# A gated delta rule layer: the last level of a block inverse in 32x32 tiles

## The chip, the cores and the metric

The kernel runs on one core of a Trainium2 chip. The metric is the device time of one execution in microseconds (us). The core has a matrix engine (PE, with its weight loads shown as PEld), a vector engine (DVE), a scalar engine (ACT), GpSimd (POOL) and a sync engine whose queue (SP) starts most transfers. Each engine works through its own list of instructions in order; engines wait for each other on semaphores.

## The reference, cut to what matters

One layer: a modulated RMS norm, one wide projection, an attention half (8 heads), a gated delta rule half (4 heads of 128), and an output projection with a gated residual. 256 tokens, float32. The change touches the delta rule alone, which works on chunks of 64 tokens:

```
sys = A + eye(64)                        # A strictly lower triangular, per head and chunk
u = solve(sys, v * beta)                 # = T (v beta),     T = inverse of sys
w = solve(sys, kb * exp(G))              # = T (kb exp G)
def step(state, xs):                     # over the 4 chunks, state starts at zero
    v_new = u_c - w_c @ state
    o     = q_c @ state + qk_c @ v_new
    state = state * gl + k_c.T @ v_new
```

For the first chunk the state is zero, so `w_c @ state` is zero and w of that chunk is used nowhere.

## The kernel before, in words

Every engine has an order of calls written out by hand; nothing is planned at run time. Tokens stand in two tiles (t = 0, 1) of 128, each with two chunks (c = 0, 1) on partitions 0 to 63 and 64 to 127. For heads 2 and 3 the two chunks of a tile stand in exchanged places; `side(h, c)` gives the partitions of chunk c of head h.

T is built by doubling blocks of 1, 2, 4, ..., 32 (`LEVELS = 6`, levels 0 to 5). `tt` holds the transpose of T as far as it is known, `am` the transposed A, `ti` the 32x32 blocks of `tt` turned on DVE. At level l and tile t:

- PE `z_products` (L1630): A times the odd blocks of T, 4 heads x 2 chunks, each with 64 contracted rows, 64 loaded columns and 32 streamed columns, into bank 2 + 2t;
- DVE `mask_z` (L1079): product with a 0/1 mask (read from `cst`) into `zt`, 128 partitions x 4 heads x 32;
- DVE `turn` (L1066): turns `tt` into `ti`;
- PE `x_products` (L1641): `ti` times `zt`, the same shapes, into the other half of the bank;
- DVE `merge` (L1086): subtracts the result from the odd blocks of `tt`.

The next level of the same tile waits for `merge` (semaphore t_done). The two tiles take turns. After level 5 come `w_products(0)`, `w_products(1)` (L1652, `kw` times `tt`, 64 contracted rows, 128 loaded and 64 streamed columns), the copies of their results by ACT (`wT_copy`, L704) and `u_products(0)` (L1666), which writes a bank that `wT_copy(0)` has to have read. Then PE goes on with units of the wide projection (`half(11)`, `half(12)`; L1395 to L1397). A product of f32 operands is issued as two MATMUL instructions, so a group of 4 heads x 2 chunks has 16.

The order around the change on PE is `x_products(4, 1)`, `z_products(5, 0)`, `z_products(5, 1)`, `x_products(5, 0)`, `x_products(5, 1)`, `w_products(0)`, `w_products(1)`, `u_products(0)`, `half(11)`, `half(12)`, `state_products(0)` (L1714), `scores(2)` (L1738). On DVE it is `merge(4, 1)`, `mask_z(5, 0)`, `turn(5, 1)`, `mask_z(5, 1)`, `merge(5, 0)`, `merge(5, 1)`, `rope(2)` (L1097, L1098, L1101), `gated_heads(1)` (L1141), `gate_sums(0, 0, 4)` (L1157), `rope(3)`, `lo(31)` (L915), `maxima(2)` (L1119, L1122), `gate_sums(0, 4, 8)`. `turn(5, 0)` stands ahead of `merge(4, 1)`. `scores(2)` waits for `rope(3)`.

Of the kernel before, what the change touches and what calls it, by code (L numbers as in the profile page):

```python
# [32 lines left out]
ACT = mybir.ActivationFunctionType  # L33
ALU = mybir.AluOpType
# [9 lines left out]
DH, DK = 4, 128  # L44
DW = DH * DK
CHUNK = 64
# [18 lines left out]
LEVELS = 6  # L65
HALF = CHUNK // 2
# [15 lines left out]
def build(nc, x, x_turned, ada, gate_w, gate_b, post_w, w_qkv, w_rest, w_gates, w_out, const, out):  # L82
    with ExitStack() as ctx:
# [73 lines left out]
        def th_array(name):  # L157
            return sb(name, [P, NTH, P])
        kw, kd, vb = th_array("kw"), th_array("kd"), th_array("vb")
        def th_block(name, n=CHUNK):  # L160
            return sb(name, [P, NTH, n])
        dec = sb("dec", [P, 2, NTH, CHUNK])
        am, qkd, qd = th_block("am"), th_block("qkd"), th_array("qd")
        ti, tt = th_block("ti"), th_block("tt")
        zt = th_block("zt", HALF)
        with ExitStack() as e:
            sq = sb("sq", [P, 4, 512], into=e)
        wT, vnew = th_array("wT"), kw
# [35 lines left out]
        z_ready, z_masked, ti_done, x_ready, t_done, wT_ready, wT_copied = map(  # L204
            sem, ("z_ready", "z_masked", "ti_done", "x_ready", "t_done", "wT_ready", "wT_copied"))
# [45 lines left out]
        def heads(a, t):  # L251
            return a[:, t * DH:(t + 1) * DH, :]

        def odd(ap, l):
            return ap.rearrange("p (n two b) -> p n two b", two=2, b=1 << l)[:, :, 1, :]

        def heads_odd(a, t, l):
            return heads(a, t).rearrange("p h (n two b) -> p (h n) two b", two=2, b=1 << l)[:, :, 1, :]

        def blocks(b, o, n):  # L260
            return bank[b][:, o:o + DH * n].rearrange("p (h j) -> p h j", h=DH)

        def rows_of(c):
            return slice(c * CHUNK, (c + 1) * CHUNK)

        def side(h, c):
            return rows_of(c if h < 2 else 1 - c)
# [4 lines left out]
        def ident_of(c):  # L272
            return ident[rows_of(c), rows_of(c)]
# [8 lines left out]
        ACROSS = (0, 2, 1, 3)  # L282
# [247 lines left out]
        def _(act):  # L530
# [169 lines left out]
            def wT_copy(t):  # L700

                act.wait_ge(wT_ready, t + 1)
                for c in range(2):
                    act.activation(heads(wT, t)[:, :, rows_of(c)], blocks(2 + 2 * t + c, 0, CHUNK), ACT.Copy, scale=-1.0).then_inc(wT_copied, 1)  # L704

            def vnew_copy(n):
                act.wait_ge(vnew_ready, n + 1)
# [109 lines left out]
            hi(29)  # L817
            hi(30)
            wT_copy(0)
            wT_copy(1)  # L820
            vnew_copy(0)
            hi(31)
# [37 lines left out]
        def _(dve):  # L860
# [215 lines left out]
            def mask_z(l, t):  # L1076

                dve.wait_ge(z_ready, NT * (l - 1) + t + 1)
                dve.tensor_tensor(heads(zt, t), blocks(2 + 2 * t, 0, HALF),  # L1079
                                  cst[:, C_LV + l * HALF:C_LV + (l + 1) * HALF].unsqueeze(1).to_broadcast([P, DH, HALF]), ALU.mult).then_inc(z_masked, 1)  # L1080

            def merge(l, t):

                dve.wait_ge(x_ready, NT * (l - 1) + t + 1)
                x_t = blocks(2 + 2 * t, 256, HALF).rearrange("p h (n b) -> p (h n) b", b=1 << l)
                dve.tensor_tensor(heads_odd(tt, t, l), heads_odd(tt, t, l), x_t, ALU.subtract).then_inc(t_done, 1)  # L1086

# [219 lines left out]
            gated_heads(0)  # L1307
            v_tokens(0)
            mask_z(1, 0)
            turn(0, 1)  # L1310
            maxima(1)
            first_pairs(1)
            turn(1, 0)
            turn(1, 1)
            mask_z(1, 1)
            merge(1, 0)
            merge(1, 1)
            turn(2, 0)
            mask_z(2, 0)
            turn(2, 1)  # L1320
            mask_z(2, 1)
            q_decayed(1)
            merge(2, 0)
            merge(2, 1)
            normalise(1)
# [66 lines left out]
        def _(pe):  # L1392
# [225 lines left out]
            def z_products(l, t):  # L1618

                b = 2 + 2 * t  # L1620
                pe.wait_ge(t_done, NT * (l - 1) + t + 1)
                if l == 1:
                    pe.wait_ge(a_done, 2 + 2 * t)
                    if t == 1:
                        pe.wait_ge(vtok_used, 1)
                for h in range(DH):
                    i = t * DH + h
                    for c in range(2):
                        r = rows_of(c)
                        ins = pe.matmul(blocks(b, 0, HALF)[r, h, :], am[r, i, :], odd(tt[r, i, :], l), start=True, stop=True)  # L1630
                ins.then_inc(z_ready, 1)

            def x_products(l, t):

                pe.wait_ge(z_masked, NT * (l - 1) + t + 1)
                pe.wait_ge(ti_done, NT * (l - 1) + t + 1)
                for h in range(DH):
                    i = t * DH + h
                    for c in range(2):
                        r = rows_of(c)  # L1640
                        ins = pe.matmul(blocks(2 + 2 * t, 256, HALF)[r, h, :], ti[r, i, :], zt[r, i, :], start=True, stop=True)  # L1641
                ins.then_inc(x_ready, 1)

            def w_products(t):
                pe.wait_ge(t_done, NT * (LEVELS - 1) + t + 1)
                pe.wait_ge(a_done, 4)
                pe.wait_ge(vtok_used, 2)
                for h in range(DH):
                    i = t * DH + h
                    for c in range(2):  # L1650
                        r = rows_of(c)
                        ins = pe.matmul(blocks(2 + 2 * t + c, 0, CHUNK)[:, h, :], kw[r, i, :], tt[r, i, :], start=True, stop=True)  # L1652
                ins.then_inc(wT_ready, 1)

            def u_products(t):
# [217 lines left out]
            kk_products(1)  # L1873
            pv(0)
            z_products(1, 0)
            scores(1)
            half(10)
            z_products(1, 1)
            x_products(1, 0)
            x_products(1, 1)  # L1880
            z_products(2, 0)
            z_products(2, 1)
            x_products(2, 0)
            x_products(2, 1)
            v_turn(1)
# [12 lines left out]
            x_products(5, 0)  # L1898
            x_products(5, 1)
            w_products(0)  # L1900
            w_products(1)
            u_products(0)
            half(11)
# [115 lines left out]
```

## Time and profile before

| | us |
|---|---|
| three runs | 190.72, 190.93 (median), 196.72 |
| the profiled execution, its own time | 190.73 |
| its span, first to last instruction | 188.9 |
| PE busy | 178.0 (94%) |
| DVE busy | 141.5 (75%) |
| ACT busy | 101.5 (54%) |
| POOL busy | 77.5 (41%) |

The span lies inside the time; the 1.8 us between the two are outside the instructions. The granted clock of PE was 0.996 of full speed on average. A MATMUL row's duration holds the pipeline's depth as well, so durations of neighbours overlap: the pace is read from the starts. In a merged row the number ahead is the start, the next the length from the first start to the last end.

### The profile page before, as it was taken

How to read it: one execution, taken by the hardware profiler on the slowest of the kernel's cores; microseconds unless marked ns; L12 is line 12 of the kernel's file. 1: busy time of each engine (PE TensorE's matmuls, PEld its weight loads, DVE VectorE, ACT ScalarE, POOL GpSimd, SP SyncE). 2: the span in 40 equal slices, each digit the busy share in tenths (PEclk: the TensorE clock that was granted, in tenths of full speed). 3: DMA queues.
4: the chain of work that ended last, by engine and by line, in shares of the span. 5: the costliest groups of instructions: out<-in, count | busy, mean ns of one | idle time of the engine just before them, and what ended most of it. 6: DMA issues, size and time to landing. Idle time of an engine off the chain costs nothing.

```text
span 188.9 us, 4380 instructions
## 1 busy us (share of the span) xinstructions
PE 178.0 (94%) x1718; PEld 161.5 (85%) x1718; DVE 141.5 (75%) x345; ACT 101.5 (54%) x195; POOL 77.5 (41%) x42
## 2 busy tenths in 40 slices
PE   7999989889999998999999999999999999999980
PEld 6769879789999998998998999999998987888850
DVE  0359699893459988998999787889689777858074
ACT  2645444439368878956562270455384448636230
POOL 2036627335687922985055068224913200810000
PEclk9999999999999999999999999999999999999998
DMA  5999999999519980300901807006942983020023
GB/s 160 403 386 394 393 409 407 407 397 404 218 16 367 395 328 8 114 0 2 323 14 17 319 8 212 13 0 220 362 201 78 344 356 119 14 97 0 3 111 111
DMA packets 12246, 38.41 MB, mean 203 GB/s; under 512 B 1473, under 2 KB 1857, under 8 KB 11714
## 3 DMA queue, kind: packets, MB, share of 16 engines
q1 hardware_dynamic: 12082, 37.61, 53.6%
q10 hardware_dynamic: 144, 0.52, 0.8%
q8 instruction: 14, 0.23, 0.5%
q14 instruction: 6, 0.05, 0.1%
HBM read 37.08 MB, written 1.05 MB: 202 GB/s over the span
## 4 chain that ended last, share of the span: by engine, by line
PE 69%; DVE 16%; DMA 6%; SPq 5%; issue 2%; ACT 1%; POOL 1%; DVEq 0%; POOLq 0%; ACTq 0%
PE bank L1395 16%; PE bank L1397 15%; PE bank L1396 15%; DVE cv L958 6%; DMA ada<-in_ada 6%; DVE bank L934 4%; SPq L351 3%; PE bank L1641 3%; PE bank L1630 3%; PE bank L1738 2%; PE bank L1745 2%; SPq L368 1%; PE bank L1754 1%; PE bank L1604 1%; PE bank L1666 1%
## 5 line engine op out<-in xcount | busy, mean ns | idle before, releaser
L474 POOL TENSOR_TENSOR wlo<-raw,whi 128x1024 fp32r<-128x1024 f32 (+1 forms) x25 | 58.1, 2334 | 62.2 <-ACT whi L543 62.2
L1395 PE MATMUL bank<-hhi,whi 128*128 128x256 f32 x218 | 63.1, 289 | 1.6 <-DVE hlo L906 1.1
L1396 PE MATMUL bank<-hhi,wlo 128*128 128x256 f32 x218 | 61.6, 283 | 0.0
L1397 PE MATMUL bank<-hlo,whi 128*128 128x256 f32 x218 | 61.6, 283 | 0.0
L1395 PEld LDWEIGHTS bank<-hhi,whi 128*128 128x128 f32 x218 | 41.7, 191 | 3.3 <-issue 1.8
L543 ACT ACTIVATE whi<-raw 128x1024 fp32r<-128x1024 f32 (+1 forms) x33 | 33.3, 1023 | 16.5 <-PE bank L1397 7.4
L1396 PEld LDWEIGHTS bank<-hhi,wlo 128*128 128x128 f32 x218 | 41.8, 192 | 0.0
L1397 PEld LDWEIGHTS bank<-hlo,whi 128*128 128x128 f32 x218 | 41.7, 191 | 0.0
L958 DVE SCALAR_TENSOR_TENSOR cv<-bank,convh,cv 128x255 f32<-128x255 f32 (+2 forms) x36 | 17.0, 481 | 5.6 <-ACT cv L609 4.6
L934 DVE SCALAR_TENSOR_TENSOR bank<-ada,sml,bank 128x256 f32<-128x256 f32 (+1 forms) x24 | 14.9, 621 | 0.7
L1157 DVE SCALAR_TENSOR_TENSOR accg<-ada,sml,accg 128x512 f32<-128x512 f32 x16 | 12.0, 751 | 2.7 <-DMA ada<-in_gate_w 2.3
L1395 PE MATMUL bank<-whi,ohi 128*128 128x512 f32 x32 | 12.6, 393 | 0.0
L1397 PE MATMUL bank<-wlo,ohi 128*128 128x512 f32 x32 | 12.5, 390 | 0.0
L672 ACT ACTIVATE pr<-bank,stat 128x128 f32<-128x128 f32 (+1 forms) x16 | 6.5, 420 | 11.1 <-DVE stat L1122 11.1
L1396 PE MATMUL bank<-whi,olo 128*128 128x512 f32 x32 | 12.4, 389 | 0.0
L915 DVE TENSOR_TENSOR wlo<-raw,whi 128x1024 fp32r<-128x1024 f32 x8 | 9.8, 1222 | 0.8 <-ACT whi L543 0.6
L488 POOL TENSOR_TENSOR rot<-rot,cst 128x512 f32<-128x512 f32 x4 | 4.4, 1092 | 12.5 <-DVE rot L1097 11.8
L1395 PE MATMUL bank<-whi,hhi 128*128 128x256 f32 x32 | 9.2, 286 | 0.0
L1396 PE MATMUL bank<-whi,hlo 128*128 128x256 f32 x32 | 9.1, 283 | 0.0
L1397 PE MATMUL bank<-wlo,hhi 128*128 128x256 f32 x32 | 9.0, 283 | 0.0
L1406 PE MATMUL bank<-ones 128*128 128x256 f32 x22 | 7.9, 530 | 1.1 <-DVE ones L868 1.1
L1406 PEld LDWEIGHTS bank<-ones 128*128 128x128 f32 x22 | 5.9, 279 | 2.3 <-DVE ones L868 1.0
(223 smaller groups left out, 337.6 us busy)
## 6 DMA issues: line engine op xcount, KB each, us to landing
raw<-in_w_rest SPq DMA_DIRECT2D x20, 512.0 KB, 4.8
ada<-in_ada SPq DMA_DIRECT2D x16, 256.0 KB, 7.1
ada<-in_ada SPq DMA_DIRECT2D x8, 512.0 KB, 12.0
ada<-in_gate_w SPq DMA_DIRECT2D x4, 1024.0 KB, 6.9
raw<-in_w_out SPq DMA_DIRECT2D x8, 512.0 KB, 5.7
raw<-in_w_qkv SPq DMA_DIRECT2D x5, 384.0 KB, 8.2
qkvs<-in_w_qkv SPq DMA_DIRECT2D x4, 384.0 KB, 11.2
cv<-in_w_qkv SPq DMA_DIRECT2D x4, 384.0 KB, 12.7
```

What stands on the lines that cost most here:

```text
L351: sp.dma_start(ada_piece(p)[:, 2 * g:2 * g + 2, :].rearrange("p k n -> p (k n)"), ada[:, o:o + n * 512]).then_inc(ada_ready(p, 2 * g)[0], 16)
L474: pool.tensor_tensor(split_u(wlo, n), raw_u(n), split_u(whi, n).bitcast(F32), ALU.subtract).then_inc(lo_done, 1)
L543: act.activation(split_u(whi, n), raw_u(n), ACT.Copy).then_inc(hi_done, 1)
L672: act.activation(pr[:, e, o:o + w], bank[ATT[e]][:, o:o + w], ACT.Exp, scale=AD ** -0.5, bias=stat[:, 16 + i:17 + i], accum_out=stat[:, 32 ...
L915: dve.tensor_tensor(split_u(wlo, n), raw_u(n), split_u(whi, n).bitcast(F32), ALU.subtract).then_inc(dve_lo_done, 1)
L934: link(dve.scalar_tensor_tensor(a, w, c_k, a, ALU.mult, ALU.add))
L958: ins = dve.scalar_tensor_tensor(cv[:, i, j:], b[:, 0:S - j], w, cv[:, i, j:], ALU.mult, ALU.add)
L1157: dve.scalar_tensor_tensor(a, adag[:, k, :], sml[:, 24 + k:25 + k], a, ALU.mult, ALU.add).then_inc(gate_acc, 1)
L1395: pe.matmul(out, a[0][ia], b[0][ib], start=start, stop=False, skip_group_check=skip)
L1396: pe.matmul(out, a[1][ia], b[0][ib], start=False, stop=False, skip_group_check=skip)
L1397: return pe.matmul(out, a[0][ia], b[1][ib], start=False, stop=stop, skip_group_check=skip)
L1406: pe.matmul(bank[b][:, 0:256], ones[:, :], ones[:, 0:1].to_broadcast([P, 256]), start=True, stop=True)
```

## The change

At level 5 the kernel works in 32x32 tiles. `z_products` loads `am` of the lower 32 partitions of the chunk (columns 0 to 31) and streams `tt` of the same partitions (columns 32 to 63), and writes the upper 32 partitions; `x_products` works on the upper 32 partitions. `mask_z` is two plain copies, one for each chunk, each 32 partitions x 4 heads x 32, without the mask; `merge` is two products with -1, of the same size, into the upper right quarter of `tt`. In `w_products(0)` the four products of the first chunk are left out (4 of 8 are left, in the order of heads 0, 2, 1, 3), and `wT_copy(0)` copies two heads instead of four in each of its two instructions. The order of the calls is not changed, nor are semaphores and transfers.

```
+        def upper(c):
+            return slice(c * CHUNK, c * CHUNK + HALF)
+        def lower(c):
+            return slice(c * CHUNK + HALF, (c + 1) * CHUNK)
...
             def wT_copy(t):
                 for c in range(2):
-                    act.activation(heads(wT, t)[:, :, rows_of(c)], blocks(2 + 2 * t + c, 0, CHUNK), ACT.Copy, scale=-1.0).then_inc(wT_copied, 1)
+                    hs = slice(0, DH) if t > 0 else slice(2 - 2 * c, 4 - 2 * c)
+                    act.activation(heads(wT, t)[:, hs, rows_of(c)], blocks(2 + 2 * t + c, 0, CHUNK)[:, hs, :], ACT.Copy, scale=-1.0).then_inc(wT_copied, 1)
...
             def mask_z(l, t):
+                if l == LEVELS - 1:
+                    for c in range(2):
+                        u = upper(c)
+                        ins = dve.tensor_copy(heads(zt, t)[u, :, :], blocks(2 + 2 * t, 0, HALF)[u, :, :])
+                    ins.then_inc(z_masked, 1)
+                    return
...
             def merge(l, t):
+                if l == LEVELS - 1:
+                    for c in range(2):
+                        u = upper(c)
+                        ins = dve.tensor_scalar(heads(tt, t)[u, :, HALF:], blocks(2 + 2 * t, 256, HALF)[u, :, :], -1.0, None, ALU.mult)
+                    ins.then_inc(t_done, 1)
+                    return
...
             def z_products(l, t):
+                        if l == LEVELS - 1:
+                            u, d = upper(c), lower(c)
+                            ins = pe.matmul(blocks(b, 0, HALF)[u, h, :], am[d, i, 0:HALF], tt[d, i, HALF:], start=True, stop=True)
...
             def x_products(l, t):
+                        if l == LEVELS - 1:
+                            u = upper(c)
+                            ins = pe.matmul(blocks(2 + 2 * t, 256, HALF)[u, h, :], ti[u, i, 0:HALF], zt[u, i, :], start=True, stop=True)
...
             def w_products(t):
-                for h in range(DH):
+                for h in ACROSS if t == 0 else range(DH):
...
+                        if t > 0 or r == side(h, 1):
+                            ins = pe.matmul(blocks(2 + 2 * t + c, 0, CHUNK)[:, h, :], kw[r, i, :], tt[r, i, :], start=True, stop=True)
```

## Rows read from the trace of the kernel before

**Rows 1.** The page: span, engines, granted clock, the chain that ended last.
```profile
span 188.9 us, 4380 instructions
PE 178.0 (94%) x1718; PEld 161.5 (85%) x1718; DVE 141.5 (75%) x345; ACT 101.5 (54%) x195; POOL 77.5 (41%) x42
PEclk9999999999999999999999999999999999999998
PE 69%; DVE 16%; DMA 6%; SPq 5%; issue 2%; ACT 1%; POOL 1%; DVEq 0%; POOLq 0%; ACTq 0%
```

**Rows 2.** Weight loads, 112 to 189 us: waited for, us, times, longest.
```profile
PEld bank L1395 <- issue: 0.8, 3, 0.3
...
PEld bank L1720 <- DVE on L1195: 0.2, 1, 0.2
```

**Rows 3.** Timeline of PE: start, length, instructions merged, levels 4 and 5 onward.
```profile
112.99 0.66 PE L1641 MATMUL bank<-zt,ti 64*64 64x32 f32 x16
...
114.87 1.21 PE L1630 MATMUL bank<-tt,am 64*64 64x32 f32 x32
115.92 1.22 PE L1641 MATMUL bank<-zt,ti 64*64 64x32 f32 x32
117.06 2.00 PE L1652 MATMUL bank<-tt,kw 64*128 64x64 f32 x32
119.02 1.09 PE L1666 MATMUL bank<-vb,tt 64*64 64x128 f32 x16
120.04 0.39 PE L1395 MATMUL bank<-hhi,whi 128*128 128x256 f32 x1
```

**Rows 4.** The same, narrow windows: the last instructions of z(5,0), x(5,0), x(5,1), w(1).
```profile
115.22 0.28 PE L1630 MATMUL bank<-tt,am 64*64 64x32 f32 x4
...
116.21 0.34 PE L1641 MATMUL bank<-zt,ti 64*64 64x32 f32 x6
...
116.79 0.34 PE L1641 MATMUL bank<-zt,ti 64*64 64x32 f32 x6
...
118.79 0.28 PE L1652 MATMUL bank<-tt,kw 64*128 64x64 f32 x2
```

**Rows 5.** Timeline of DVE, level 5 of both tiles and what follows.
```profile
115.09 0.29 DVE L1086 TENSOR_TENSOR tt<-tt,bank 128x128 f32<-128x128 f32 x1 [0.35 <-PE bank L1641]
115.55 0.29 DVE L1079 TENSOR_TENSOR zt<-bank,cst 128x128 f32<-128x128 f32 x1 [0.18 <-PE bank L1630]
115.76 0.44 DVE L1066 STREAM_TRANSPOSE ti<-tt 128x256 f32<-128x256 f32 x1
116.13 0.29 DVE L1079 TENSOR_TENSOR zt<-bank,cst 128x128 f32<-128x128 f32 x1
116.60 0.29 DVE L1086 TENSOR_TENSOR tt<-tt,bank 128x128 f32<-128x128 f32 x1 [0.18 <-PE bank L1641]
117.18 0.29 DVE L1086 TENSOR_TENSOR tt<-tt,bank 128x128 f32<-128x128 f32 x1 [0.29 <-PE bank L1641]
117.40 0.73 DVE L1097 STREAM_SHUFFLE rot<-bank 128x512 f32<-128x512 f32 x1
```

**Rows 6.** Groups of DVE instructions by shape, whole span: short ones and plain copies.
```profile
L1177 DVE COPY state<-bank 128x256 f32<-128x256 f32 x2 | 0.7, 416 | 0.0
...
L1052 DVE TENSOR_TENSOR am<-bank,dec 128x256 f32<-128x256 f32 x2 | 0.8, 420 | 0.4 <-PE bank L1614 0.4
...
L1006 DVE COPY gcs<-bank 128x32 f32<-128x32 f32 x1 | 0.2, 191 | 0.0
```

**Rows 7.** Timeline of ACT after the w products.
```profile
118.22 0.66 ACT L704 ACTIVATE wT<-bank 128x256 f32<-128x256 f32 x2 [4.46 <-PE bank L1652]
```

**Rows 8.** Timeline of DVE from `gate_sums(0, 0, 4)` to `maxima(2)`.
```profile
120.39 3.11 DVE L1157 SCALAR_TENSOR_TENSOR accg<-ada,sml,accg 128x512 f32<-128x512 f32 x4
...
125.50 0.69 DVE L1101 TENSOR_TENSOR kT<-rot 128x512 f32<-128x512 f32 x1 [0.76 <-POOL rot L488]
126.11 1.22 DVE L915 TENSOR_TENSOR wlo<-raw,whi 128x1024 fp32r<-128x1024 f32 x1
127.41 0.30 DVE L1119 CUSTOM_DVE_ANT_0 bank<-bank,cst 128x128 f32<-128x128 f32 x1
...
128.81 0.90 DVE L1122 SCALAR_TENSOR_TENSOR stat<-stat,ones 128x4 f32<-128x4 f32 x1
129.64 3.10 DVE L1157 SCALAR_TENSOR_TENSOR accg<-ada,sml,accg 128x512 f32<-128x512 f32 x4
```

**Rows 9.** Timeline of PE around `scores(2)`, and POOL beside it.
```profile
125.98 0.72 PE L1714 MATMUL bank<-kw,kd 64*128 64x128 f32 x8
126.53 0.82 PE L1738 MATMUL bank<-kT,qT 64*128 64x128 f32 x8
...
127.29 2.41 POOL L474 TENSOR_TENSOR wlo<-raw,whi 128x1024 fp32r<-128x1024 f32 x1 [1.89 <-ACT whi L543]
```

**Rows 10.** Stretches: us, busy of PE, PEld, DVE, ACT, POOL, clock, DMA share, GB/s.
```profile
0.00:2.00 2.00, 0.95 (x2) 0.84 (x3) 0.19 (x4) 0.84 (x1) 1.15 (x5) 1.00 0.10 17
...
114.83:115.35 0.52, 0.52 (x24) 0.52 (x20) 0.26 (x1) 0.00 (x0) 0.52 (x2) 1.00 0.76 307
...
185.00:188.00 3.00, 0.00 (x0) 0.00 (x0) 1.49 (x3) 0.00 (x0) 0.00 (x0) 0.91 0.46 170
```

More of the change, by code:

```diff
@@ L1629, in z_products @@
                         r = rows_of(c)
-                        ins = pe.matmul(blocks(b, 0, HALF)[r, h, :], am[r, i, :], odd(tt[r, i, :], l), start=True, stop=True)
+                        if l == LEVELS - 1:
+                            u, d = upper(c), lower(c)
+                            ins = pe.matmul(blocks(b, 0, HALF)[u, h, :], am[d, i, 0:HALF], tt[d, i, HALF:], start=True, stop=True)
+                        else:
+                            ins = pe.matmul(blocks(b, 0, HALF)[r, h, :], am[r, i, :], odd(tt[r, i, :], l), start=True, stop=True)
                 ins.then_inc(z_ready, 1)
@@ L1639, in x_products @@
                     for c in range(2):
-                        r = rows_of(c)
-                        ins = pe.matmul(blocks(2 + 2 * t, 256, HALF)[r, h, :], ti[r, i, :], zt[r, i, :], start=True, stop=True)
+                        if l == LEVELS - 1:
+                            u = upper(c)
+                            ins = pe.matmul(blocks(2 + 2 * t, 256, HALF)[u, h, :], ti[u, i, 0:HALF], zt[u, i, :], start=True, stop=True)
+                        else:
+                            r = rows_of(c)
+                            ins = pe.matmul(blocks(2 + 2 * t, 256, HALF)[r, h, :], ti[r, i, :], zt[r, i, :], start=True, stop=True)
                 ins.then_inc(x_ready, 1)
@@ L1651, in w_products @@
                         r = rows_of(c)
-                        ins = pe.matmul(blocks(2 + 2 * t + c, 0, CHUNK)[:, h, :], kw[r, i, :], tt[r, i, :], start=True, stop=True)
+                        if t > 0 or r == side(h, 1):
+                            ins = pe.matmul(blocks(2 + 2 * t + c, 0, CHUNK)[:, h, :], kw[r, i, :], tt[r, i, :], start=True, stop=True)
                 ins.then_inc(wT_ready, 1)
```

## The prediction

> **What bounds the kernel now.** I read the page first: PE is busy for 94% of the span and makes up 69% of the chain that ended last [rows 1]. Then the waits of the weight loads from 112 us on: in those 77 us only one short wait, 0.2 us, is put down to another engine; the others have nothing behind them but issue [rows 2]. So from level 5 of the inverse to the end at 183 us a microsecond that PE is given goes to the end of the kernel, and one that it loses too, unless a later wait takes it back. Then the timelines of PE and DVE through level 5 [rows 3, 5]. PE looks full there, but DVE is the pace: every DVE row starts 0.05 us after the end of a PE group, and PE's next group starts about 0.05 us after DVE's. For instance merge(4,1) ends at 115.09 + 0.29 = 115.38, and z(5,1) starts at 115.43. Last, the DVE rows after the inverse: from 117.40 on DVE has no wait for PE until rope(3) ends at 125.50 + 0.69 = 126.19 [rows 5, 8], and scores(2) waits for it. It first multiplies at 126.53 and its weights load 0.11 earlier, at 126.42 [rows 9]; with 0.05 for the signal it could have started 0.18 us earlier. That 0.18 us is the slack on which this forecast turns.
>
> **Pace on PE.** Pace is (length of the row - duration of one) / (count - 1). z and x, 64 loaded and 32 streamed columns: (0.66 - 0.22) / 15 = 29 ns for each instruction. w, 128 loaded and 64 streamed: (2.00 - 0.27) / 31 = 56 ns. u, 64 loaded and 128 streamed: (1.09 - 0.27) / 15 = 55 ns [rows 3]. Loads and streams run beside each other and the longer sets the pace: 64 columns more to load cost 27 ns (56 against 29), 128 streamed ones cost 55. A 32x32 tile loads 32 columns, 29 - 13.5 = 16 ns, and streams 32, 55 / 4 = 14 ns. I take 16 ns, since both rows lead there; the other bound is no gain, 29 ns. A group of 16 then takes 0.25 us in place of 0.47. The Trainium skill speaks against the first bound: "TensorEngine Tiling (Array Packing)", Instruction Overhead, says a matmul has some 60 cycles of overhead and that no tiling factor should be taken from a dimension that is already small. By that the pace would hardly move; the sum for it is the first rival's.
>
> **Cost of the additional mode.** x(5,1) starts its last instruction at 116.79 + 0.34 - 0.22 = 116.91 and w(0), of another tile shape, starts at 117.06, 0.15 later, where groups of one shape follow at 0.05 [rows 3, 4]. Part of it may be the wait for merge(5,0) (116.89 + 0.05 = 116.94), so a change of shape costs 0 to 0.10 us. The change adds one, ahead of z(5,0); I take 0.10. The skill's same page, Key Properties, says that a change of tiling mode drains the engine; that agrees with the upper value.
>
> **DVE.** mask and merge are two instructions each instead of one, four more in all. A DVE instruction occupies the engine from its start to the next one's: 115.76 - 115.55 = 0.21 us for 128x128, 0.37 for the turn [rows 5]. The new ones have as many elements per partition (4 x 32) on a quarter of the partitions. No row has fewer partitions. A plain copy from a bank takes as long as a product of the same shape, 416 against 420 ns, and one of 32 elements still takes 191 ns, of which about 0.1 would be occupation [rows 6]. So an additional one costs 0.1 to 0.27 us; I take 0.21, the row with the same elements per partition. That the mask is no longer read is worth nothing by the same comparison.
>
> **The stretch, step by step** (before in brackets; all starts from [rows 3 to 5]):
> - z(5,0) starts at 114.97 (114.87), ends 0.24 + 0.22 later at 115.43 (115.50). z(5,1) waits for merge(4,1), unchanged at 115.43.
> - mask(5,0) starts at 115.48 (115.55); its second copy ends at 115.48 + 0.21 + 0.29 = 115.98. x(5,0) starts at 116.03 (115.92).
> - The turn follows at 115.90, mask(5,1) at 116.27 (116.13), ending 116.77; x(5,1) starts at 116.82 (116.48).
> - x(5,0) ends at 116.03 + 0.46 = 116.49, but DVE is free only at 116.27 + 0.42 = 116.69: merge(5,0) ends at 117.19, and w(0) starts at 117.24 (117.06).
> - x(5,1) ends at 117.28; merge(5,1) starts at 117.33, ends at 117.83, and DVE goes on to rope(2) at 117.75 (117.40). **DVE is 0.35 us later.**
> - w(0) has 8 instructions less, 8 x 0.056 = 0.45 us: 0.94 - 0.45 = 0.49, so PE is free at 117.73 but w(1) needs merge(5,1): 117.88 (118.00). With 0.05 for the restart, its last instruction starts at 118.72 (118.79), and u starts 0.15 later for the change of shape: 118.87 (119.02).
> - wT_copy(0) is off that path: w(0) ends near 117.9, and even two full copies, 0.66 us [rows 7], end at 118.6. Before, they ended at 118.88, which held u by up to 0.08.
>
> So PE comes out of the inverse **0.15 us earlier**: the 0.45 us of the omitted products and the quicker tiles are eaten by 4 x 0.21 us of DVE.
>
> **What is late next.** half(11), half(12) and state_products(0) carry the 0.15 us to scores(2), which PE could start at 126.42 - 0.15 = 126.27. rope(3) is 0.35 us late and signals at 126.59. So scores(2) starts 0.32 us after PE is there and 126.59 - 126.42 = **0.17 us later than before**. Queued behind it on PE are half(13) and all that follows. On DVE lo(31) and maxima(2) are late too, but the small L1122 ended at 129.71, with POOL's subtraction of 2.41 us from 127.29 (end 129.70), and took 0.90 us there [rows 8, 9]. It has 0.74 us of cover, so gate_sums(0,4,8), and the transfer that waits for it, don't move by the 0.35. No transfer is moved in a queue, neither SP's nor POOL's, and POOL has no instruction more.
>
> **Sum.** -0.15 (PE out of the inverse) turned into +0.17 at scores(2); nothing later gives it back. The profiled execution took 190.73, so 190.90. The median of the runs is 0.20 above it, at 190.93; I forecast 191.0, between 190.90 and 191.10.
>
> **Rivals.**
> 1. *The small tiles are no quicker* (29 ns). z(5,0) then ends at 115.60 and mask(5,0) starts at 115.65, 0.17 later than above; x(5,1) starts at 116.99 and ends at 117.68 and rope(2) starts at 117.73 + 0.42 = 118.15, 0.75 late. scores(2) signals at 126.99: +0.57, 191.3 by the profile's time, 191.5 by the median. For it: no row has so small a tile. Against: both rows of larger tiles scale with their columns. Here PE also leaves the inverse later than before (w(1) starts at 118.28), so it is slower everywhere.
> 2. *Short DVE instructions are cheap* (0.1 us each additional). The two additional masks and the first merge then move x(5,1) to 116.60 and rope(2) to 117.42, late by at most 0.05; w(1) starts at 117.55, 0.45 earlier, and scores(2), ready at 126.29, starts 0.13 earlier: 190.6 by the profile's time. With a signal that is not late at all -0.18 is the most that scores(2) allows, and a quarter of a microsecond more only if DVE gained too: 190.3. For it: the 191 ns row. Against: that row has 32 elements per partition, not 128.
> 3. *PE's clock falls* (slower). After the change PE stands still in four places between z(5,0) and w(1), each under 0.5 us. If that let the clock fall to 1.2 from 2.4 GHz for half(11) and half(12) (120.0 to 126.0), those 6 us would become up to 12 and the time up to 197; with half of that stretch, 194. Against: the granted clock was 1.00 even in the first 2 us, where PE was busy for 0.95 of 2.00, and fell only to 0.91 where PE had ended altogether [rows 10].
> 4. *The change does something else than it says*: with the small tiles not taken as such, it is rival 1.
>
> **How the numbers follow.** Forecast 50%, rival 1 (with 4) 20%, rival 2 26%, rival 3 4%, half of that over 2%. The terms' bounds (pace 16 or 29 ns, 0 to 0.10 us for the shape, 0.1 to 0.27 us for each DVE instruction) give 190.3 to 191.7, of which single runs spread 0.2 to either side: 190.1 to 191.8. About 2% is what a measurement of this kernel can tell from no change, with one of three runs 3% above the others. Faster by over 2% asks for 3.8 us, and the whole of level 5, w and u is 5.2: 1%. Slower by over 2%: 3%. Within 2%: 96%.
>
> **What would show it.** Right: MATMUL rows of 32*32 at 16 ns pace; PE idle ahead of x(5,1), put down to the copies; rope(2) starting near 117.75; u near 118.9; scores(2) with a wait of 0.3 us for L1101. Wrong: a pace of 29 ns; additional DVE instructions that occupy 0.1 us; scores(2) without a wait; a granted clock under 1.00 between 115 and 127 us.

## The result, and the profile after

The changed kernel takes 194.73 us (median of 4 runs, 194.42 to 195.44); the kernel before, run beside it, 191.36 (190.72 to 196.72, 4 runs). The ratio of the runs is 1.0199, with an interval of 1.0177 to 1.0222: slower by 2%. Ratios, here and below, leave out the runs over 1.5% above the fastest of their kernel, which the kernel before has beside every set of runs (here 196.72), and the experiments in one run of e1 (198.62), two of e3 (195.45 and 197.59), three of e4 (195.34 to 199.22), one of e8 (201.23) and four of e12 (194.02 to 197.07). The forecast was 191.0, with 190.1 to 191.8 as its range. The profiled execution took 194.58 us, 3.85 more than before's 190.73.

The page of the changed kernel, the lines that answer to [rows 1]. The third is PE's granted clock in 40 slices of 4.8 us, in tenths:

```profile
span 192.8 us, 4368 instructions
PE 180.1 (93%) x1710; PEld 162.7 (84%) x1710; DVE 142.6 (74%) x349; ACT 101.3 (53%) x195; POOL 77.6 (40%) x42
PEclk9999999999999999999999996699999999999996
```

Two slices in the middle stand at 6, where before had 9. PE has 8 instructions less and is busy for 2.1 us more. Now the stretches of the changed kernel (us; busy of PE, PEld, DVE, ACT, POOL; granted clock; DMA share and GB/s):

```profile
115.40:116.02 0.62, 0.40 (x16) 0.29 (x16) 0.57 (x3) 0.00 (x0) 0.62 (x1) 1.00 0.04 13
116.02:116.46 0.44, 0.44 (x16) 0.33 (x16) 0.43 (x1) 0.00 (x0) 0.44 (x1) 1.00 1.12 158
116.46:117.11 0.65, 0.00 (x1) 0.00 (x1) 0.59 (x3) 0.00 (x0) 0.65 (x1) 1.00 0.58 120
117.11:117.50 0.39, 0.39 (x16) 0.33 (x16) 0.38 (x2) 0.00 (x0) 0.39 (x1) 1.00 0.85 347
117.50:117.72 0.22, 0.05 (x4) 0.00 (x0) 0.19 (x2) 0.00 (x0) 0.00 (x0) 0.52 0.99 410
...
122.40:124.20 1.80, 1.80 (x10) 1.80 (x9) 1.73 (x3) 0.76 (x2) 0.00 (x0) 0.50 0.00 0
124.20:124.40 0.20, 0.20 (x3) 0.20 (x2) 0.20 (x1) 0.00 (x0) 0.00 (x0) 0.67 0.00 0
124.40:127.00 2.60, 2.60 (x24) 2.60 (x23) 0.56 (x3) 0.54 (x1) 0.00 (x0) 1.00 0.00 0
```

PE stands still for 0.22 us ahead of x(5,0), for 0.65 ahead of x(5,1) and for 0.17 ahead of w(0). At about 117.5, at the end of x(5,1) and just ahead of the third gap, its clock falls to half, 1.2 GHz in place of 2.4, and it comes back at about 124.3. So two gaps, 0.22 and 0.65 us, stand before the fall. The timelines of PE and then of DVE through the same stretch, which answer to [rows 3, 5]:

```profile
114.90 0.90 PE L1651 MATMUL bank<-tt,am 32*32 32x32 f32 x32
116.02 0.44 PE L1665 MATMUL bank<-zt,ti 32*32 32x32 f32 x16 [0.22 <-DVE zt L1089]
117.11 0.44 PE L1665 MATMUL bank<-zt,ti 32*32 32x32 f32 x16 [0.65 <-DVE zt L1089]
117.72 2.83 PE L1680 MATMUL bank<-tt,kw 64*128 64x64 f32 x24 [0.17 <-DVE tt L1101]
120.48 1.97 PE L1694 MATMUL bank<-vb,tt 64*64 64x128 f32 x16
...
129.72 0.82 PE L1766 MATMUL bank<-kT,qT 64*128 64x128 f32 x8
```

```profile
115.02 0.29 DVE L1105 TENSOR_TENSOR tt<-tt,bank 128x128 f32<-128x128 f32 x1 [0.35 <-PE bank L1668]
115.39 0.58 DVE L1089 COPY zt<-bank 32x128 f32<-32x128 f32 x2
116.00 0.45 DVE L1073 STREAM_TRANSPOSE ti<-tt 128x256 f32<-128x256 f32 x1
116.48 0.58 DVE L1089 COPY zt<-bank 32x128 f32<-32x128 f32 x2
117.09 1.20 DVE L1101 TENSOR_SCALAR tt<-bank 32x128 f32<-32x128 f32 x4
...
118.32 0.73 DVE L1116 STREAM_SHUFFLE rot<-bank 128x512 f32<-128x512 f32 x1
```

Two things are to be seen. A pair of new DVE instructions takes the engine for 0.61 us (115.39 to 116.00), where one instruction had taken 0.21 [rows 5]; rope(2) starts at 118.32, 0.92 later than before. And u, 16 instructions, takes 1.97 us at half the clock where it took 1.09 [rows 3], while w, with 8 instructions less, takes 2.83 where it took 2.00.

Where the 3.85 us come in is read from PE's rows further on: the first products of vnew(1), then scores(3), first before and then in the changed kernel.

```profile
136.11 0.66 PE L1679 MATMUL bank<-state,wT 128*64 128x128 f32 x8
146.49 0.89 PE L1738 MATMUL bank<-kT,qT 64*128 64x128 f32 x8
```

```profile
139.29 0.66 PE L1707 MATMUL bank<-state,wT 128*64 128x128 f32 x8
150.25 0.93 PE L1766 MATMUL bank<-kT,qT 64*128 64x128 f32 x8 [0.40 <-DVE stg L1160]
```

PE is 3.18 us late at vnew(1) and 3.80 late at the end of scores(3) (151.18 against 147.38), where it has waited once more for DVE.

### The profile page after: what moved, and what is told of

The parts are those of the page before. It is cut to its first block and busy times, and to the rows that moved or that the text cites. A ratio compares the mean times of both kernels' runs of the same rounds, so it can differ in the third digit from the quotient of the medians.

```text
span 192.8 us, 4368 instructions
## 1 busy us (share of the span) xinstructions
PE 180.1 (93%) x1710; PEld 162.7 (84%) x1710; DVE 142.6 (74%) x349; ACT 101.3 (53%) x195; POOL 77.6 (40%) x42
## 5 line engine op out<-in xcount | busy, mean ns | idle before, releaser
L480 POOL TENSOR_TENSOR wlo<-raw,whi 128x1024 fp32r<-128x1024 f32 (+1 forms) x25 | 58.7, 2357 | 60.9 <-ACT whi L549 60.8
L1425 PE MATMUL bank<-ones 128*128 128x256 f32 x22 | 7.1, 485 | 1.1 <-DVE ones L875 1.1
L480 POOL TENSOR_TENSOR wlo<-cv,whi 128x768 fp32r<-128x768 f32 x3 | 5.5, 1861 | 5.1 <-ACT whi L549 5.1
```

Of the source, the lines that this page charges most:

```text
L480: pool.tensor_tensor(split_u(wlo, n), raw_u(n), split_u(whi, n).bitcast(F32), ALU.subtract).then_inc(lo_done, 1)
L1425: pe.matmul(bank[b][:, 0:256], ones[:, :], ones[:, 0:1].to_broadcast([P, 256]), start=True, stop=True)
```

## The experiments

Theory A: PE's standing still in level 5 let the clock fall, and the late DVE costs some 0.7 us more at scores(2). Theory B: the small tiles themselves don't keep the clock up, or it is DVE's lateness that costs the time. Twelve kernels ran; the ratios are against the kernel before, on the same chip, and the clock is the mean granted clock of the profiled run.

| kernel | profiled run, us | clock in it | ratio | interval |
|---|---|---|---|---|
| the change | 194.58 | 0.973 | 1.0199 | 1.0177 to 1.0222 |
| e1_filler | 191.53 | 0.995 | 1.0048 | 1.0030 to 1.0065 |
| e2_dve_split | 193.43 | 0.983 | 1.0100 | 1.0023 to 1.0177 |
| e3_w_only | 191.26 | 0.993 | 1.0026 | 1.0012 to 1.0039 |
| e4_one_dve | 192.64 | 0.989 | 1.0034 | 0.9994 to 1.0075 |
| e5_real_work | 198.85 | 0.978 | 1.0436 | 1.0391 to 1.0481 |
| e6_combined | 195.13 | 0.983 | 1.0224 | 1.0197 to 1.0251 |
| e7_w_and_order | 199.43 | 0.979 | 1.0414 | 1.0376 to 1.0451 |
| e8_full_w | 194.03 | 0.989 | 1.0208 | 1.0133 to 1.0283 |
| e9_w_early_gate | 196.09 | 0.987 | none | |
| e10_tiles_early_gate | 196.02 | 0.983 | 1.0287 | 1.0257 to 1.0317 |
| e11_w_lo35_early | 190.81 | 0.996 | 0.9976 | 0.9966 to 0.9987 |
| e12_lo35_early | 190.83 | 0.990 | 0.9987 | 0.9974 to 0.9999 |

**e1_filler: keep PE busy, change nothing else.**

```
             z_products(5, 1)
+            filler(1)
             x_products(5, 0)
+            filler(2)
             x_products(5, 1)
+            filler(1)
             w_products(0)
```

`filler` issues matmuls of ones, 128x128, whose result is not used.

> The changed kernel, with matmuls of ones into a free part of bank 6 (their results are not used) in the places where PE stood still: one ahead of x(5,0), two ahead of x(5,1), one ahead of w(0). Theory A (the clock fell because PE stood idle for 0.22 + 0.65 us): granted clock 1.00 from 114 to 128 us; what is left is DVE's lateness, rope(2) at 118.3 instead of 117.4, so scores(2) about 0.74 late: 191.5 us. Theory B (the small 32x32 tiles themselves don't count as work for the clock, or the lateness of DVE costs the time): still near 194.5, clock 0.5 after 117.5.

Measured: 191.53 us in the profiled run, against an expected 191.5; the nine runs of the ratio lie between 191.42 and 192.28, 0.9 us over before. Its stretches (columns as above), and the wait that its weight loads show at scores(2):

```profile
116.00:117.00 1.00, 1.00 (x21) 0.84 (x21) 0.93 (x4) 0.00 (x0) 1.00 (x1) 1.00 0.61 82
117.00:118.00 1.00, 1.00 (x21) 0.73 (x19) 0.93 (x4) 0.00 (x0) 0.56 (x1) 1.00 0.89 356
118.00:119.00 1.00, 1.00 (x19) 0.98 (x18) 0.95 (x4) 0.27 (x2) 0.00 (x0) 1.00 0.22 86
```

```profile
PEld bank L1766 <- DVE kT L1120: 0.3, 1, 0.3
```

```profile
127.26 0.93 PE L1766 MATMUL bank<-kT,qT 64*128 64x128 f32 x8
136.93 0.66 PE L1707 MATMUL bank<-state,wT 128*64 128x128 f32 x8
147.31 0.83 PE L1766 MATMUL bank<-kT,qT 64*128 64x128 f32 x8
```

The clock stays at 1.00 and 3.05 us of the 3.85 are gone, with four more matmuls on PE and all the rest as in the change. What is left, 0.80, is DVE: scores(2) starts at 127.26, 0.73 later than before, and waits for L1120, the end of rope(3), and vnew(1) is 0.82 late. The 3.05 have two parts. Up to vnew(1) the changed kernel loses 2.36 us to this one (139.29 against 136.93): that is PE at half the clock. The other 0.7 come at scores(3), where the changed kernel waits 0.40 us and this one doesn't. The changed kernel's second gate load took 5.43 us from its issue to DVE's use (135.94 to 141.37), this one's 4.67 (133.67 to 138.34). No run shows that the clock had a part in that; e3 below has the same wait with its clock up. So the clock is shown to cost 2.4 us, and 3.05 with the wait that came with it.

Theory A expected this result. Theory B's two reasons, small tiles or DVE's lateness, were both still there and the clock stayed up. But the filler is work of full size as well as an end to the gaps, and e1 doesn't separate the two.

**e2_dve_split: the DVE part alone, with the old tiles.**

`mask_z` and `merge` of level 5 are two instructions each on 32 partitions, as in the change; PE keeps its 64x64 tiles and all w products.

> The kernel before, with only the mask and the merge of level 5 each split into two DVE instructions of 32 partitions; PE keeps its 64x64 tiles and all w products. Both theories expect 0.3 us for each such instruction, so rope(2) about 0.9 us late. Theory A: PE idles about 0.6 us ahead of x(5,1), as in the changed kernel, and the clock falls: 194.5 to 195.5 us. Theory B (small tiles): clock stays 1.00, 191.3 to 191.7 us.

Four runs: 193.43, 192.19, 192.19 and 194.56 us, with mean clocks of 0.983, 0.996, 0.996 and 0.977. In the profiled one PE stands still ahead of x(5,1) for 0.43 us and the clock falls later than in the change, and for half as long:

```profile
119.50:120.30 0.80, 0.80 (x17) 0.73 (x15) 0.70 (x2) 0.57 (x3) 0.53 (x1) 1.00 0.00 0
120.30:123.50 3.20, 3.20 (x23) 2.87 (x22) 2.47 (x5) 1.35 (x4) 0.56 (x1) 0.51 0.02 5
123.50:124.00 0.50, 0.50 (x5) 0.50 (x4) 0.50 (x1) 0.00 (x0) 0.00 (x0) 0.73 0.00 0
```

So 32x32 tiles are not needed for the fall. Nor does it come in every run, by the mean clocks: the two runs at 0.996 take 192.19, 1.1 us over before. These have no trace; that this is the late DVE is likely from e1's 0.8 and not shown.

**e3_w_only: the cut w products alone.**

```
 w_products(t):
-                for h in range(DH):
+                for h in ACROSS if t == 0 else range(DH):
...
+                        if t > 0 or r == side(h, 1):
```

The copies of w(0) by ACT are halved too, as in the change.

> The kernel before, with only the four unused w products of the first chunk left out and the copies of w(0) halved. Both theories: clock stays 1.00; u starts 0.4 us earlier, but scores(2) can start at most 0.18 us earlier since it waits for rope(3): 190.5 to 190.8 us, same within noise.

It missed: 1.0026, slower and not faster. u starts early (118.48) and scores(2) at 126.16, 0.37 before [rows 9], with its end 0.26 before, and yet the kernel's end is later. The loss stands at scores(3). PE's row there, and DVE's rows ahead of it:

```profile
146.83 0.93 PE L1740 MATMUL bank<-kT,qT 64*128 64x128 f32 x8 [0.43 <-DVE stg L1142]
```

```profile
137.95 3.11 DVE L1158 SCALAR_TENSOR_TENSOR accg<-ada,sml,accg 128x512 f32<-128x512 f32 x4 [2.86 <-DMA ada<-in_gate_w]
140.99 0.42 DVE L1146 TENSOR_TENSOR olo<-stg,ohi 128x256 fp32r<-128x256 f32 x1
141.32 3.11 DVE L1158 SCALAR_TENSOR_TENSOR accg<-ada,sml,accg 128x512 f32<-128x512 f32 x4
144.35 1.22 DVE L916 TENSOR_TENSOR wlo<-raw,whi 128x1024 fp32r<-128x1024 f32 x1
```

The second gate load is issued at 132.57 and DVE can use it at 137.95, 5.38 us later. In the kernel before it is 132.77 to 137.58, 4.81 us. From there DVE has no idle time until gated_heads(2) (L1142), for which scores(3) waits. A PE that is ahead only waits there. The forecast had not looked past scores(2). The changed kernel has the same wait, 0.40 us at 150.25. Why the load took 0.57 us longer here is not shown.

**e4_one_dve: the change with one DVE instruction each.**

```
 merge, level 5 (in words and code):
-  two dve.tensor_scalar(..., -1.0, None, ALU.mult) on 32 partitions
+  dve.scalar_tensor_tensor(tt[:, :, HALF:], x, mask column, tt[:, :, HALF:], ALU.mult, ALU.subtract, reverse1=True)
 mask_z, level 5: the masked product of before
```

> The changed kernel with mask and merge of level 5 as one DVE instruction each on all 128 partitions (the merge multiplies by the 0/1 column of the mask). 32x32 tiles and the cut w products stay. Theory A: PE idles 0.1 to 0.3 us at a time, clock stays 1.00, rope(2) at 117.3 to 117.5, and scores(2) 0.1 to 0.2 us earlier than before: 190.4 to 190.9 us. Theory B (small tiles): clock falls after 117 us, 193.5 to 194.5 us.

The seven runs of the ratio lie apart: 190.59, 190.90 and 191.42 us with mean clocks of 0.997 to 0.999, 191.49 with 0.983, and 192.64, 192.76 and 192.83 with 0.989 to 0.990. The profiled run is of the last kind:

```profile
115.78 0.97 PE L1657 MATMUL bank<-zt,ti 32*32 32x32 f32 x32
116.67 1.63 PE L1672 MATMUL bank<-tt,kw 64*128 64x64 f32 x24
118.23 1.96 PE L1686 MATMUL bank<-vb,tt 64*64 64x128 f32 x16
```

```profile
118.30:121.70 3.40, 3.40 (x24) 3.07 (x24) 2.57 (x6) 1.42 (x4) 0.73 (x1) 0.50 0.02 7
```

DVE is on time (rope(2) at 117.07), PE is busy for 3.29 of the 3.40 us from 114.90 to 118.30, and the clock still falls for 3.4 us in this run. Theory A in its plain form (idle time alone) doesn't cover that: here the clock falls with next to no idle time among short small-tile products. Theory B in its plain form (small tiles bring the fall whatever stands beside them) is refuted by e1.

**e5_real_work: bulk work in the gaps.** `half(11)` is issued in pieces of three matmuls: one ahead of x(5,0), two ahead of x(5,1), one ahead of w(0), the other four behind u.

> The changed kernel with four of the eight pieces of half(11) (each six bulk matmuls, 0.36 us, that PE has to do anyway) put in the places where PE stood still: one ahead of x(5,0), two ahead of x(5,1), one ahead of w(0). Theory A (idle time let the clock fall; DVE's lateness costs 0.7 us at scores(2)): clock 1.00 from 112 to 128 us, scores(2) at about 127.3 as with the filler, although PE reaches it earlier: 191.5 us. Rival (the small tiles keep the clock down): 194 us and more, clock 0.5 after 118.

(A piece is three matmuls, not six; its 0.36 us is right.) The clock is 1.00 from 112 to 128 us, as theory A has it; but the time is 198.85, far over the expected 191.5. DVE and POOL in that kernel:

```profile
127.71 3.39 DVE L922 TENSOR_TENSOR wlo<-raw,whi 128x1024 fp32r<-128x1024 f32 x1
...
144.36 5.08 DVE L1176 SCALAR_TENSOR_TENSOR accg<-ada,sml,accg 128x512 f32<-128x512 f32 x4
149.36 1.21 DVE L922 TENSOR_TENSOR wlo<-raw,whi 128x1024 fp32r<-128x1024 f32 x1
```

```profile
127.12 2.90 POOL L480 TENSOR_TENSOR wlo<-raw,whi 128x1024 fp32r<-128x1024 f32 x1
...
146.39 2.50 POOL L480 TENSOR_TENSOR wlo<-raw,whi 128x1024 fp32r<-128x1024 f32 x1 [5.98 <-ACT whi L549]
```

lo(31) on DVE takes 1.22 us when alone [rows 8] and 3.39 here, with its end (131.1) a microsecond behind that of POOL's subtraction (130.0); four gate_sums take 3.11 alone and 5.08 across the second one. Both engines' instructions read two operands from SBUF, and in these rows DVE stands until POOL is done. With PE and POOL ahead and DVE behind, they meet. scores(2) waits 1.31 us and scores(3) 3.76, and in the second gap the clock falls as well (0.59 from 150 to 155 us); over the first it stayed at 1.00.

**e6_combined and e7_w_and_order: three moves meant to free the gain.** scores(2) behind half(13), gate_sums(0, 4, 8) ahead of maxima(2), v_copy(1) ahead of probs(2); e6 with the tiles, one DVE instruction each and pieces of half(11), e7 with the old tiles; both with the cut w products.

> A version meant to be faster than both: 32x32 tiles and the cut w products, one DVE instruction each for mask and merge, three pieces of half(11) in PE's gaps, scores(2) behind half(13), and on DVE gate_sums(0, 4, 8) ahead of maxima(2), so that the second load of the gate weights starts about 2 us earlier (on ACT v_copy(1) goes ahead of probs(2)). Theory A (PE bound once neither clock, nor rope(3), nor the gate load holds it): PE has 0.45 us less w and 4 x 0.21 us less level 5, minus some 0.3 us for changes of tile shape: 189.8 us, 189.5 to 190.3. Rival (another wait of the same kind takes its place, or the clock falls): 190.7 us or more.

> The kernel before with the cut w products and the same three moves (scores(2) behind half(13), gate_sums(0, 4, 8) ahead of maxima(2), v_copy(1) ahead of probs(2)); 64x64 tiles. If what cost e3_w_only its 0.45 us was the late landing of the second gate load (gated_heads(2) held scores(3) for 0.43 us), the gain now arrives: 190.3 us. If the cut w products don't pay for another reason: 190.9 us or more.

Both missed, at 1.0224 and 1.0414. In e7 gate_sums(0, 4, 8) meets POOL's subtraction at 127 us and takes 5.25 us in place of 3.10, the next groups 5.26 and 5.07; PE waits 1.64 us ahead of vnew(1) and 3.98 at scores(3). Over e7's first gap, 1.64 us behind bulk products, the clock stayed at 1.00; it fell only in the second. e6 keeps its clock at 1.00 through level 5, which is one more case for theory A's remedy, and loses 2.25 us ahead of vnew(1); behind that gap its clock does fall (0.50 from 139.5 to 141 us). In e6 the piece of half(11) ahead of x(5,0) starts at 115.72 and x(5,0) at 116.27: 0.55 us for 0.36 of work, so the change of shape behind it takes some 0.2.

**e8_full_w: the change with all w products.**

```
-  if t > 0 or r == side(h, 1):       # and the half copies of w(0)
+  all eight products, full copies
```

> The changed kernel with all eight w products and the full copies of w(0) back. If the clock falls because of the idle time in level 5, it falls here too, at about 117.6 us, and w costs 0.45 us more, twice that at half the clock: 195.2 to 195.6 us. If the cut w products had a part in it (less work for PE in that stretch), the clock stays up or falls later and shorter: 191.5 to 193 us.

Between the two expectations: 1.0208, with runs of 194.03, 195.14 and 196.16 us at clocks of 0.989, 0.981 and 0.968. In the profiled run the gaps are the same (0.22, 0.65, 0.17), but the clock falls later, at about 119.9, and is back at about 123.3. So the fall doesn't need the cut products. Whether they had a part in when it came and how long it lasted, as the second expectation had it, is open: the other two runs have lower mean clocks than the profiled one and no trace.

**e9_w_early_gate and e10_tiles_early_gate.** e9 is e3 with rope(3) ahead of the fourth gate_sums instruction and the first half of the second gate load waiting for four of them in place of eight; e10 the same with tiles, one DVE instruction each and three pieces of half(11).

> The kernel before with the cut w products (64x64 tiles, DVE untouched at level 5), and two moves that take away the waits which ate the gain of e3_w_only: rope(3) goes ahead of the fourth gate_sums instruction (which follows lo(31)), so that scores(2) doesn't wait; and the first half of the second gate load waits for four gate_sums instructions instead of eight, so that it is issued about 2 us earlier. DVE's lo(31) still starts ahead of POOL's subtraction. If PE is the bound once these waits are gone: scores(2) 0.5 us earlier than before, scores(3) without a wait for L1141, ratio 0.997 to 0.998 (190.4 against 191.0). If another wait takes their place, or the moved gate_sums instruction falls under POOL's subtraction and loses 2 us: ratio 1.00 or above.

> As e9_w_early_gate, but with the 32x32 tiles, one DVE instruction each for mask and merge, and three pieces of half(11) (three bulk matmuls each) in PE's gaps. If the small tiles had something to give once their gaps are filled: 0.4 us and more under e9. In e6_combined a piece of 0.36 us took 0.55 us with the changes of tile shape on both sides, and u came 3.62 us after z(5,0) with 1.08 us of other work done, against 3.70 in e3_w_only with none, so PE has 1.1 us in hand; against it, DVE reaches rope(2) 0.6 us later, and POOL's subtraction can start ahead of lo(31) on DVE. My expectation: clock 1.00 throughout and a ratio of 0.995 to 1.00 if the collision doesn't happen, 1.02 or more if it does, as in e5_real_work.

Both missed. Five of e9's six runs took 195.1 to 196.1 us and one 191.16; they lie too far apart for a ratio. The profiled one, 196.09, shows where its time goes. DVE, then POOL:

```profile
139.29 3.12 DVE L1158 SCALAR_TENSOR_TENSOR accg<-ada,sml,accg 128x512 f32<-128x512 f32 x4 [3.31 <-DMA ada<-in_gate_w]
...
145.68 3.37 DVE L916 TENSOR_TENSOR wlo<-raw,whi 128x1024 fp32r<-128x1024 f32 x1
```

```profile
145.21 2.77 POOL L474 TENSOR_TENSOR wlo<-raw,whi 128x1024 fp32r<-128x1024 f32 x1 [7.00 <-ACT whi L543]
```

The gate load, issued at 131.28 instead of 132.77, is there later (139.29): 8.01 us in place of 4.81, 0.5 us behind the issue of the load before it where there had been 2.7. Why it took so long is not shown. So lo(35) starts 0.5 us after POOL's subtraction instead of 1.0 ahead of it, and takes 3.37 us. scores(3) waits 3.42. e10, at 1.0287, shows the same meeting, DVE and then POOL:

```profile
145.57 3.37 DVE L922 TENSOR_TENSOR wlo<-raw,whi 128x1024 fp32r<-128x1024 f32 x1
```

```profile
145.38 2.48 POOL L480 TENSOR_TENSOR wlo<-raw,whi 128x1024 fp32r<-128x1024 f32 x1 [6.00 <-ACT whi L549]
```

Its scores(3) waits 3.13 us. In its level 5 the clock stayed at 1.00, small tiles and all.

**e11_w_lo35_early and e12_lo35_early: take lo(35) out of the way.**

```
 DVE:
+            lo(35)
             gate_sums(1, 0, 4)
             heads_lo(1)
             gate_sums(1, 4, 8)
-            lo(35)
 ACT: hi(35) goes ahead of pT_copy(2)
```

e12 is that alone, e11 that with the cut w products.

> The kernel before with the cut w products, and with lo(35) on DVE moved from behind the second gate_sums group to ahead of it, into the 2.3 us in which DVE waits for the second gate load (hi(35) on ACT goes ahead of pT_copy(2)). In e3_w_only scores(3) waited 0.43 us for gated_heads(2), because the gate load landed 0.6 us later after its issue than before; in e9 lo(35) fell under POOL's subtraction and cost 2.1 us more. If these DVE waits are all that ate the cut products' 0.45 us, scores(3) now comes 0.3 us earlier than before and the ratio is 0.997 to 0.999; scores(2), which waits for rope(3), keeps the gain under 0.37 us. If DVE meets POOL's subtraction here too, 1.00 to 1.01.

> The kernel before with the same move of lo(35) and hi(35) alone, all w products kept, as the reference for e11_w_lo35_early: PE is the bound there, so the same as before, ratio 0.999 to 1.001. If it is faster, the move has a gain of its own; if the cut products are worth nothing at all, e11 equals it.

e11: 0.9976 (0.9966 to 0.9987), all 12 runs between 190.36 and 190.88 us. It is faster than the kernel before, by 0.24%, and than the change. e12: 0.9987 (0.9974 to 0.9999). The two intervals overlap, so the share of the cut products, some 0.1%, is not resolved; what is shown is that they no longer cost anything. In e11 scores(3) doesn't wait. Its level 5 begins 0.32 us later than before (z(5,0) at 115.19 against 114.87), its scores(3) only 0.13 later (146.62 against 146.49), so some 0.2 us of the 0.45 arrive there:

```profile
137.49 1.34 DVE L916 TENSOR_TENSOR wlo<-raw,whi 128x1024 fp32r<-128x1024 f32 x1 [1.99 <-ACT whi L543]
138.76 3.10 DVE L1158 SCALAR_TENSOR_TENSOR accg<-ada,sml,accg 128x512 f32<-128x512 f32 x4
...
145.91 0.42 DVE L1142 SCALAR_TENSOR_TENSOR stg<-bank,gm 128x256 f32<-128x256 f32 x1
```

## Why the prediction was wrong

**What bounds the kernel: right, and too short.** PE carries what it gains or loses to the end, and scores(2) with its 0.18 us of slack was the next wait. e1 bears this out: rope(3) ends 1.01 us later than before (127.20 against 126.19), less 0.18 is 0.83, and vnew(1) is 0.82 late. But the reading stopped there. The wait of scores(3) for gated_heads(2), which had at most 0.19 us of slack (L1141 ends at 146.30, scores(3) multiplies at 146.49), was not looked at; e3 lost its gain on it.

**Pace on PE: right.** (0.90 - 0.19) / 31 = 23 ns over both z groups with the wait between them, and x alone (0.44 - 0.19) / 15 = 17 ns, against 16 forecast. Rival 1 is refuted. The Trainium skill's page "TensorEngine Tiling (Array Packing)", Instruction Overhead, would have had the pace hardly move for so small a dimension; by these rows it went from 29 to 17 ns, so the measurement decides against it here. Rows and columns of the tile shrank together, and no run separates them.

**Cost of the additional shape: right.** z(5,0) starts 0.15 us after the last x instruction (114.31 + 0.66 - 0.22 = 114.75, then 114.90), as taken.

**DVE: mis-sized, beyond the bound.** An additional instruction was put at 0.21 us, at most 0.27. It takes 0.29 to 0.31: 0.61 for a pair, and the turn behind a pair occupies 0.48 instead of 0.37. Back to back instructions on 128 partitions overlap by some 0.08 us [rows 5]; these don't. The second of a pair also starts at another partition (64 and not 0); whether that or the smaller number of partitions takes the overlap away was not tried. Four additional ones and the slower turn came to 0.92 us at rope(2) in place of 0.35. By the forecast's own rule for scores(2) that is 0.74 in place of 0.17, and 191.5 in place of 191.0; e1, with 0.99 at rope(2), measured 191.53.

**The clock: the step that failed.** Rival 3 named the mechanism, the place and a price (a stretch at half the clock from level 5 into half(11)), and got 4%. The argument against it was that the clock stood at 1.00 in the first 2 us with PE busy for 0.95 of them [rows 10]. A row from the kernel's first microseconds says nothing of the middle, where PE stood still twice within 2 us between short products before the fall. One of the gaps was 0.65 us, and the forecast had 0.33 there and none over 0.5: the mis-sized DVE instructions made it longer. The size is measured by e1: 194.58 - 191.53 = 3.05 us, of which 2.36 are PE's at half the clock and the rest the wait at scores(3). The low stretch is 6.8 us long (117.5 to 124.3) and half of that, 3.4, is what it could cost at most. From w(0) to state_products(0) the changed kernel takes 11.45 us and e1 8.44, 3.01 less; e1 gives 0.30 of them back by starting w(0) later, behind its filler, and 0.35 by its wait at scores(2) and the longer row there.

**w products and what is late next.** That they save 0.45 us on PE is right (u at 118.48 in e3, 119.02 before, with level 5 begun 0.09 earlier). That it goes into a later wait was right in kind for scores(2). The cover in L1122, by which gate_sums(0,4,8) and the gate load would not move, was not there. The small instruction ends when POOL's subtraction does, and that moved too. In e1 POOL, behind the later lo(31), ends at 130.60 instead of 129.70; gate_sums(0,4,8) starts at 130.55 instead of 129.64 and the gate load is issued at 133.67 instead of 132.77.

**What stays open.** What makes the clock fall is not settled. Together, gaps and small tiles brought the fall in the profiled run of the change and, by their mean clocks of 0.973 to 0.974, in its other three. Gaps with the old tiles (e2) did in two of four, small tiles with 0.11 us of gaps in all (e4) in some, the profiled one among them. Work of full size in the gaps (e1, e5, e6, e10) kept it away. Idle time alone is not the measure: 1.31 us (e5) and 1.64 us (e7) of standing still further on, where the products use 64 to 128 rows, left the clock at 1.00, and in the change 0.22 and 0.65 between short ones did not; behind 2.25 us (e6) it fell. So the little work that the short products give PE seems to count, but no run holds the gaps fixed and changes only the products between them.

## What to carry to other kernels

Before an instruction of an engine off the path is split in two, ask what the busiest engine does meanwhile: 0.22 and 0.65 us of standing still in the middle of short products cost 2.4 us through the clock, where DVE's lateness itself cost under one. When time is saved on the bounding engine, follow every wait on other engines to the end of the kernel and note its slack; two of them here, with 0.18 and at most 0.19 us, held a saving of 0.45. And take the engine that the gain runs into out of the way first (e11), then make the cut.

## What the runs showed of the hardware

- The granted clock fell to half behind gaps of 0.22 and 0.65 us between 32x32 products (the change), and in e4's profiled run with PE idle for 0.11 us in the 3.40 us before. It stayed at 1.00 over gaps of 1.31 us (e5, ahead of 64x128 products) and 1.64 us (e7, behind 128x128 ones).
- DVE instructions with two SBUF operands that started behind a GpSimd subtraction of 128x1024 stood still until it was done: 3.37 to 3.39 us in place of 1.22 (e5, e9, e10), and a group of four 5.1 to 5.3 in place of 3.1 (e5, e7). With lo(31) on DVE ahead, it took its 1.22 us and POOL's subtraction 2.76 to 2.83 in place of 2.41 (e3, e1). In these runs the one that started first went ahead, and 1.5 us of shift was enough to turn it.
- Pairs of DVE instructions on 32 partitions (0.284 us each, 128 elements per partition, starting at partitions 0 and 64) followed each other at 0.29 to 0.31 us, those on 128 partitions (0.29 each) at 0.21.
- Matmuls on 32x32 tiles have a duration of 191 to 194 ns, against 219 on 64x64 tiles, and a pace of 17 against 29 ns.
- A load issued 1.5 us earlier was there for DVE 1.7 us later, 8.01 us after its issue in place of 4.81 (e9).
